# Each expert's row gathered in two halves, in an encoder step with a mixture of 16,384 rank-one experts

## What is computed

```
q = (xb @ w_pq).reshape(t, 8, 2, 128);  s = einsum('thpd,phkd->thpk', q, keys)
top 16 of each half, top 16 of the 256 sums  ->  expert (t, 8, 16), best_s
g = softmax(best_s)
h = einsum('td,thkd->thk', xb, u_emb[expert])
act = g * gelu(h)
out = einsum('thk,thkd->td', act, v_emb[expert])
```

## Time and profile before

| what | value |
| --- | --- |
| median of 3 runs | 3346.39 us (3346.24 to 3348.15) |
| the profiled execution, own time | 3345.38 us |
| its span, first to last instruction | 3343.4 us |
| busy: PE, DVE, POOL, ACT | 2485.5, 2445.1, 1397.8, 1033.0 us |
| gathers | 1,088 of 1 MB |
| mean granted TensorE clock | 0.869 |

### The profile page before, as it was taken

One profiled execution on the slowest core, in us unless ns is written; L12 is line 12 of the kernel. 1 busy time (PEld: TensorE's weight loads), 2 busy tenths in 40 slices (PEclk: granted clock), 3 DMA queues, 4 the chain that ended last, 5 costly groups with the idle time before them and its releaser, 6 DMA issues. The chain is left out here.

```text
span 3343.4 us, 41075 instructions
## 1 busy us (share of the span) xinstructions
PE 2485.5 (74%) x13555; PEld 1077.4 (32%) x13555; DVE 2445.1 (73%) x6920; ACT 1033.0 (31%) x2944; POOL 1397.8 (42%) x1266
## 2 busy tenths in 40 slices
PE   8999766777867776678767876787767766776665
PEld 4555522333322332233323332333323222222221
DVE  4888677668777777777777777777677777677885
ACT  3333233333332323332333233323332233222321
POOL 1222344344444444434444443544434444444453
PEclk9999778889887899889888988888889888888877
DMA  6223399999999999999999999999999999999997
GB/s 200 79 79 93 106 396 408 381 362 409 414 414 401 411 410 410 399 408 408 409 392 408 407 402 404 397 408 401 402 407 407 409 411 413 373 402 417 414 419 314
DMA packets 221480, 1220.90 MB, mean 365 GB/s; under 512 B 34370, under 2 KB 62738, under 8 KB 82005
## 3 DMA queue, kind: packets, MB, share of 16 engines
q0 software_dynamic: 156672, 1140.92, 84.3%
q1 hardware_dynamic: 61072, 75.91, 6.8%
q10 hardware_dynamic: 3525, 1.45, 0.2%
HBM read 1199.65 MB, written 18.55 MB: 364 GB/s over the span
## 5 line engine op out<-in xcount | busy, mean ns | idle before, releaser
L1241 POOL DMA_INDIRECT uv_rows<-in_uv_emb,experts x1088 | 1260.8, 1159 | 1629.0 <-PE ps L1349 1422.5
L1349 PE MATMUL ps<-uv_rows,diag 64*64 64x512 f32 x8704 | 1334.4, 738 | 812.4 <-ACT diag L1645 811.4
L1878 DVE CUSTOM_DVE_ANT_0 uv_rows<-uv_rows,handed 128x1024 f32<-128x1024 f32 x1088 | 1329.9, 1224 | 608.1 <-DMA uv_rows<-in_uv_emb,experts 602.8
L1349 PEld LDWEIGHTS ps<-uv_rows,diag 64*64 64x64 f32 x8704 | 322.9, 153 | 1458.5 <-ACT diag L1645 1034.0
L1637 ACT ACTIVATE gelu_c<-dots 128x2 f32<-128x2 f32 x544 | 110.5, 203 | 1606.4 <-DVE dots L1878 1606.0
L1645 ACT ACTIVATE diag<-ident_twice,act_c 128x64 f32<-128x64 f32 x1088 | 319.2, 340 | 281.5 <-DVE act_c L1895 280.3
L1309 PE MATMUL ps<-w_pq_sb,xnT_c 128*128 128x256 f32 x1152 | 339.3, 425 | 0.7 <-ACT xnT_c L1604 0.7
L1309 PEld LDWEIGHTS ps<-w_pq_sb,xnT_c 128*128 128x128 f32 x1152 | 217.9, 206 | 249.0 <-issue 226.2
L653 DVE SCALAR_TENSOR_TENSOR handed<-w_out_sb,tapsT,handed 128x128 f32<-128x128 f32 x960 | 252.8, 351 | 0.0
L590 PE MATMUL ps<-w_in_sb,w_out_sb 128*128 128x512 f32 (+1 forms) x656 | 240.7, 522 | 0.5 <-DMA w_in_sb<-in_w_in 0.5
L1895 DVE SCALAR_TENSOR_TENSOR act_c<-gelu_c,gate_inv,gate_exps 128x2 f32<-128x2 f32 x544 | 118.2, 217 | 77.0 <-ACT gelu_c L1637 57.6
(11 more groups left out here) (248 smaller groups left out, 2166.8 us busy)
## 6 DMA issues: line engine op xcount, KB each, us to landing
uv_rows<-in_uv_emb,experts POOLq DMA_INDIRECT x1088, 12.9
w_in_sb<-in_w_in SPq DMA_DIRECT2D x4, 2048.0 KB, 15.6
w_pq_sb<-in_w_pq SPq DMA_DIRECT2D x8, 1024.0 KB, 6.7
w_out_sb<-in_x_prompt SPq DMA_DIRECT2D x8, 512.0 KB, 4.3
w_out_sb<-in_w_out SPq DMA_DIRECT2D x1, 4096.0 KB, 16.4
handed<-in_x_prompt SPq DMA_DIRECT2D x8, 512.0 KB, 17.1
out<-handed SPq DMA_DIRECT2D x8, 512.0 KB, 7.9
keys_turned<-handed SPq DMA_DIRECT2D x10, 260.0 KB
```

The source lines that it names most:

```text
L1241: nc.gpsimd.indirect_dma_start(out=rows[:, m % RING, :], out_offset=None, in_=d.uv_emb[0], in_offset=bass.IndirectOffsetOnAxis(ap=experts[ ...
L1349: ins = pe.matmul(ps[dst, 2 * x + half, :], diag[src, (m + i) % DIAGS, :], rows[src, (m + i) % RING, cols], start=first, stop=last)
L1878: nc.vector.tensor_tensor_reduce(out=row, in0=row, in1=xn[:, block_of(n) % 2, :], scale=1.0, scalar=0.0, op0=ALU.mult, op1=ALU.add, accum_ ...
```

## The change

- The joined table `uv_emb` is gone; `u_emb` and `v_emb` are passed as they are. The ring of 8 slots of 8 KB becomes two rings of 8 slots of 4 KB, in the same memory.
- POOL issues two indirect DMAs a step, of 128 rows of 4 KB each: the `u` half of step `m`, which waits only for dot `m - 8`, and the `v` half of step `m - 2`, which waits until step `m - 10` has been weighed. DVE waits for the `u` half, PE for the `v` halves of its pair.
- Block 1's output projection is spread, one matmul a step, over item 4 from step 9 to item 5 step 10, and what follows from it (sum, mean square, normalisation, turned rows, queries of items 8 and 9) moves back by up to an item. The queries, scores and copies of items 8 and 9 get their own places in items 6 and 7.

```diff
@@ phase_c
-        rows = sb("uv_rows", [P, RING, 2 * s.D])
+        u_rows = sb("u_rows", [P, RING, s.D])
+        v_rows = sb("v_rows", [P, RING, s.D])
...
         def routed_in(n):
-            return chosen_in(n + 1)
+            return {6: [8], 7: [9, 10]}.get(n, chosen_in(n + 1))
@@ POOL
             def gather(n, k):
                 m = K * n + k
                 if m >= RING:
+                    pool.wait_ge(dot_done, m - RING + 1)
+                nc.gpsimd.indirect_dma_start(
+                    out=u_rows[:, m % RING, :], out_offset=None, in_=d.u_emb[0],
+                    in_offset=bass.IndirectOffsetOnAxis(ap=experts[:, slot_of(n), k:k + 1], axis=0),
+                ).then_inc(u_here[m % RING], 16)
+
+            def gather_values(m):
+                if m >= RING:
                     pool.wait_ge(weighed, (m - RING) // 2 + 1)
                 nc.gpsimd.indirect_dma_start(
-                    out=rows[:, m % RING, :], out_offset=None, in_=d.uv_emb[0],
-                    in_offset=bass.IndirectOffsetOnAxis(ap=experts[:, slot_of(n), k:k + 1], axis=0),
-                ).then_inc(here[m % RING], 16)
+                    out=v_rows[:, m % RING, :], out_offset=None, in_=d.v_emb[0],
+                    in_offset=bass.IndirectOffsetOnAxis(ap=experts[:, slot_of(m // K), m % K:m % K + 1], axis=0),
+                ).then_inc(v_here_ring[m % RING], 16)
...
                 for k in range(K):
                     gather(n, k)
+                    if K * n + k >= LAG:
+                        gather_values(K * n + k - LAG)
...
-                    if n == 5 and k == 15:
+                    if n == 6 and k == 7:
                         inverse_rms1(1)
+            for m in range(K * HEADS - LAG, K * HEADS):
+                gather_values(m)
@@ PE
             def weigh(n, k):
                 m, b = K * n + k, block_of(n)
+                for i in range(2):
+                    pe.wait_ge(v_here_ring[(m + i) % RING], 16 * ((m + i) // RING + 1))
...
-                                            rows[src, (m + i) % RING, cols], start=first, stop=last)
+                                            v_rows[src, (m + i) % RING, cols], start=first, stop=last)
...
-                    if n == 4 and 9 <= k < 13 or n == 5 and k < 4:
-                        for i in range(2):
-                            project(1, 2 * (k - 9 if n == 4 else k + 4) + i)
-                    if n == 5 and k == 6:
+                    if n == 4 and k >= 9:
+                        project(1, k - 9)
+                    if n == 5 and k == 0:
+                        project(1, 7)
+                    if n == 5 and 3 <= k < 11:
+                        project(1, k + 5)
+                    if n == 5 and k == 14:
                         gains(1, 0)
-                    if n == 5 and k == 11:
+                    if n == 6 and k == 2:
                         gains(1, 1)
...
+                    if n == 6:
+                        if 8 <= k < 12:
+                            query(8, 2 * (k - 8), 2 * (k - 7))
+                        if k == 12:
+                            turn_query(8)
+                        if k == 14:
+                            score(8)
+                        if k == 15:
+                            query(9, 0, 4)
@@ DVE
             def dot(n, k):
                 m = K * n + k
-                dve.wait_ge(here[m % RING], 16 * (m // RING + 1))
+                dve.wait_ge(u_here[m % RING], 16 * (m // RING + 1))
...
-                row = rows[:, m % RING, 0:s.D]
+                row = u_rows[:, m % RING, :]
...
-                    if n == 4 and k == 13:
+                    if n == 5 and k == 2:
                         projected(1, 0)
-                    if n == 5 and k == 4:
+                    if n == 5 and k == 12:
                         projected(1, 1)
-                    if n == 5 and k == 5:
+                    if n == 5 and k == 13:
                         mean_square1(1)
-                    if n == 5 and k == 6:
+                    if n == 5 and k == 14:
                         mean_scaled1(1)
-                    if n == 5 and k == 9:
+                    if n == 6 and k == 1:
                         normalise1(1, 0)
-                    if n == 5 and k == 12:
+                    if n == 6 and k == 4:
                         normalise1(1, 1)
```

More of the change, by code:

```diff
@@ L79, in build @@
 def build(nc, x_prompt, x_sample, cache_k, cache_v, cache_logf, state_conv, g_mix, w_in, b_f, w_dw, b_dw,
-          ln_g, ln_b, w_out, g_ffn, w_pq, sub_keys, uv_emb, g_final,
+          ln_g, ln_b, w_out, g_ffn, w_pq, sub_keys, u_emb, v_emb, g_final,
           y_prompt, y_sample, k_prompt, v_prompt, logf_prompt, conv_prompt,
           k_sample, v_sample, logf_sample, conv_sample):
-    s = sizes(x_prompt, x_sample, cache_k, w_in, w_dw, w_pq, sub_keys, uv_emb)
+    s = sizes(x_prompt, x_sample, cache_k, w_in, w_dw, w_pq, sub_keys, u_emb)
     d = Named()
@@ L86, in build @@
     d.g_mix, d.w_in, d.b_f, d.w_dw, d.b_dw, d.ln_g = g_mix, w_in, b_f, w_dw, b_dw, ln_g
-    d.ln_b, d.w_out, d.g_ffn, d.w_pq, d.sub_keys, d.uv_emb = ln_b, w_out, g_ffn, w_pq, sub_keys, uv_emb
+    d.ln_b, d.w_out, d.g_ffn, d.w_pq, d.sub_keys, d.u_emb, d.v_emb = ln_b, w_out, g_ffn, w_pq, sub_keys, u_emb, v_emb
     d.g_final, d.k_prompt, d.v_prompt, d.logf_prompt, d.conv_prompt = g_final, k_prompt, v_prompt, logf_prompt, conv_prompt
@@ L1002, in phase_c @@
         RING = 8
+        LAG = 2
         DIAGS = 6
@@ L1082, in phase_c @@
         best_ready, exps_ready, experts_ready, pair_ready = sem("best_ready"), sem("exps_ready"), sem("experts_ready"), sem("pair_ready")
-        here = [sem(f"uv_here{i}") for i in range(RING)]
+        u_here = [sem(f"u_here{i}") for i in range(RING)]
+        v_here_ring = [sem(f"v_here{i}") for i in range(RING)]
         dot_done, weighed = sem("dot_done"), sem("weighed")
@@ L1344, in weigh @@
                         pe.wait_ge(crossed_out, 2 * (b - 1) + half + 1)
-                    cols = slice(s.D + half * BANK, s.D + (half + 1) * BANK)
+                    cols = slice(half * BANK, (half + 1) * BANK)
                     for i in range(2):
@@ L1561, in _ @@
                         turn_rows(made_in(n, 3), (k - 7) // 4)
[L1562 to L1565 removed]
+                    if n == 4 and k >= 9:
[5 more added lines that the diff above has]
+                    if n == 5 and k == 14:
                         gains(1, 0)
[L1567 removed]
+                    if n == 6 and k == 2:
                         gains(1, 1)
[L1569 to L1572 removed]
+                    if n == 6 and k in (5, 7):
+                        turn_rows(1, (k - 5) // 2)
                     if left and k == 1:
                         score(left[0])
[L1575 removed]
+                    if n == 6:
[7 more added lines that the diff above has]
+                            query(9, 0, 4)
+                    elif len(routed) == 1:
                         if n > 0 and k in (1, 3, 5, 7):
@@ L1581, in _ @@
                             score(routed[0])
-                    if len(routed) == 2:
+                    if n == 7:
+                        if k == 1:
+                            query(9, 4, 8)
+                        if k == 3:
+                            turn_query(9)
+                        if k == 5:
+                            score(9)
+                    elif len(routed) == 2:
                         if k in (1, 3):
@@ L1588, in _ @@
                             score(routed[0])
+                    if len(routed) == 2:
                         if k in (9, 11):
@@ L1767, in _ @@
                         rows_out(made_in(n, 3), (i - 4) // 2)
-                    if (n, i) in ((5, 7), (6, 0)):
-                        rows_out(1, n - 5)
+                    if n == 6 and i in (3, 4):
+                        rows_out(1, i - 3)
                     head_step(n, i)
-                    if len(routed) == 1:
+                    if n == 6:
+                        if i == 5:
+                            query_out(8)
+                        if i == 6:
+                            turned_out(8)
+                        if i == 7:
+                            scores_out(8)
+                    elif len(routed) == 1:
                         if i == 4:
@@ L1778, in _ @@
                     if len(routed) == 2:
-                        if i == 2:
+                        early = 1 if n == 7 else 0
+                        if i == 2 - early:
                             query_out(routed[0])
-                        if i == 3:
+                        if i == 3 - early:
                             turned_out(routed[0])
-                        if i == 4:
+                        if i == 4 - early:
                             scores_out(routed[0])
@@ L2135 @@
 INPUTS = ["x_prompt", "x_sample", "cache_k", "cache_v", "cache_logf", "state_conv", "g_mix", "w_in", "b_f", "w_dw",
```

(2 more changed lines are left out.)

12 lines of the change are left out of this document (3 added, 9 removed).

## The result

The changed kernel takes **3545.16 us** (median of 4 runs, 3535.69 to 3551.41) against 3346.66 before on the same chip: **1.0591 times as long, 95% interval 1.0574 to 1.0608**. The profiled execution took 3549.35 us, 4.2 above the median, with a span of 3547.6. Forecast were 3470, in a range from 3405 to 3620: the direction and the new bound came out as forecast, the size was 75 us short.

A forecast was written before the change was run, and what follows sets the result against it. Transfers were taken to bound the kernel before, POOL's issues the changed one: 3345.4 + 1,088 x (2.782 - 2.667) - 2 = 3468.5, with 1.0 for the median about 3470 us, range 3405 to 3620.

The forecast's parts named there:

- The transfers bound the kernel before: Phase C before the change: about five gathers always under way, ring full, one landing every 2.667 us, so transfers limit.
- block 1's holes: DMA share gaps around block 1's projection: 11.5 of 15 us of holes; filling them gives back 12, between 0 and 15.
- The spread projection gives nothing where POOL is the bound: Block 1's projection: filling its holes gives nothing once POOL is the bound, since POOL has no slack.
- Packets of 4 KB, 114 us: Gather transfers: 4 KB rows at 403 GB/s against 8 KB at 420, 0.105 us a step, 114 us over 1,088 steps.
- The two ends, nothing and 123: Other bounds on added packets: nothing if only bytes count; 123 us at 12.6 ns for each of 9,792 packets.
- the 3445 of the rival: Rival: transfers remain the bound and POOL keeps up, 3445 us, from 3405 to 3455; chance 0.34.
- the 3405: Lower end of the transfer-bound rival and of the forecast range, given as packets at 7 ns.
- The fixed cost of a DMA: Skill's rule of about 2.0 us a DMA: 2,176 us more if nothing overlapped; given no chance of its own.
- POOL becomes the bound, 2.78 us a step, 1.09 us an issue: POOL's two issues a step, held up by dots, set the pace; forecast 3470 us, case 3455 to 3620, chance 0.49.
- What would show it: Signs: 4 KB packets near 400 GB/s at share 1.0, or holes; POOL over 75% busy; DVE's `u` wait up.
- I cost the shift at nothing: `v` halves two steps late, some 5.3 us, delaying PE's weighing: 0 us, absorbed by DVE's 603 us of gather waits.
- worse still: Rival: DVE's waits on PE come on top, 3470 + 181 = 3651 us, above 3620; chance 0.08.

The follow-up runs named there:

- e4_short_dot: Changed kernel with each dot over the first 256 of 1,024 columns, the rest left out; 3393.86 us, ratio 1.0148.
- e5_spread_short_dot: Kernel before (joined 8 KB rows) with block 1's projection spread and dots over 256 of 1,024 columns; 3331.11 us, ratio 0.9948.
- e11_weigh_later: Changed kernel, lag of two steps kept, with PE's weighing of each pair two steps later in PE's order; 3442.83 us, ratio 1.0275.
- e3_half_bytes: Changed kernel with gathers of 2 KB a row in place of 4 KB, dots whole; 3672.72 us, ratio 1.0977.
- e7_two_issues: Kernel before with each gather made two DMAs of 64 rows of 8 KB, one to each half of the partitions; 5497.87 us, ratio 1.6432.

## Why the prediction was right, and where not

- **The transfers bound the kernel before.** Right. Filling block 1's holes gives 11.5 us by itself (forecast 12), and shorter dots give another 3.5 to 7 and no more.
- **The spread projection gives nothing where POOL is the bound.** Right: whole change and halves alone differ by 1.5 us, within their spread.
- **Packets of 4 KB, 114 us.** Mis-sized: 63 measured. The two ends, nothing and 123, hold it. The 403 against 420 GB/s of the earlier trace rows came from stretches of 9 and 40 us, and the faster one was the last items, where little else moves; in the long run it is 398 in `e4_short_dot` against 407 in `e5_spread_short_dot`. With 63 the transfers alone would have ended near 3334.6 + 63 = 3398, under the 3445 of the rival, so POOL was further above the transfers than "close". Two slips in these sums change nothing: the 3405 is packets at 7.5 ns, not 7 (which makes 3400), and 2.761 / 2 - 0.30 is 1.0805, not 1.079.
- **The fixed cost of a DMA.** 1,088 more DMAs, with all their packets, cost 63 us. The 2,176 us estimated from the Trainium skill, "DMA: Bandwidth & Descriptors", section "Anatomy of one DMA — SWDGE (gpsimd) path", do not show.
- **POOL becomes the bound, 2.78 us a step, 1.09 us an issue.** The mechanism is right: an issue that starts in a dot is held until 0.8 us after it, and nearly every dot catches one. An issue takes 1.110, a step 2.852. With the lag's effect taken away it is sized well: in `e11_weigh_later`, whose dots are as even as the prediction assumed or more so, the dots pace at (3426.9 - 429.0) / 1087 = 2.758. Some luck is in that: the prediction counted three issues for any long interval; with one more for each further 1.25 us the kernel before comes to 1.951 issues a dot, and the pace to 2.73. Against the transfer-bound 3394 this hold-up by evenly spaced dots costs 49 us.
- **What would show it.** POOL is busy 2126.6 of the 2,700 us from 500 to 3200, 79%, and no longer waits for weighing, as forecast. Two signs did not come: no holes appeared in the DMA share, which stayed at 1.00 with the rate at 375 GB/s in the place of about 400, and DVE's wait for `u` halves went down, from 603 us to 440, since DVE came late itself.
- **The step that failed: "I cost the shift at nothing while DVE has its 603 us of waiting for gathers to absorb it."** It measured 80 us when the lag was taken away, 102 when the weighing was moved instead. Counted in DVE's time the sentence is true: it is busy 68% of the span, and still waits 440 us for gathers. But the cover was argued for DVE's own delay, and the price came through another engine. The late `v` halves make PE late, PE makes DVE late, the dots bunch, and bunched dots hold up POOL, which has no slack. The pace of 2.78 was worked out with the dots spaced as before, and the same change that made POOL the bound took that spacing away. The forecast of 3470 is 27 us above the 3443 measured with even dots, and has nothing for the 102: that makes the 75 by which it was short. The rival "worse still" had the first two links right, but bounded it at one step for each item, 181 us, as a delay in DVE's order.

The sum as measured: 3334.6 (whole rows, projection spread) + 63 (packets) + 49 (even dots against POOL) + 102 (uneven dots, through the lag and the place of the weighing) = 3548.6. It is a way of dividing the time, and no test: the terms are differences of the same runs, and come out at 3545.2 but for the 3.5 that short dots give the joined rows as well (3334.6 against 3331.1), from which the 63 are counted. The runs were made on several chips, on which the kernel before took 3346.1 to 3349.4 us, and single runs of one of these kernels lie 2 to 28 us apart, so none of the terms is sharper than some 5 us, and the last than some 10.

What stays open: how much of the 102 is the lag's alone, since weighing later was not tried without lag; and whether two issues a step could be had without any cost through dots, that is with DVE reading its rows in another way. It wasn't tried.

## What to carry to other kernels

Before an issuing engine's work is doubled, work out its pace with its real mean duration, the hold-ups by other engines in it, and not from the median of an undisturbed issue; and ask whether the change also moves the engine that holds it up. An engine with idle time need not absorb a delay for nothing: here the delay made its work bunch, and the price was paid by POOL, which the bunch holds up. When data are made to arrive later, move the instruction that waits for them back by as much in its queue, for everything behind it waits too: that alone gave back half of what the change lost.

## What the runs showed of the hardware that was not expected

- **A DMA share of 1.00 is no proof that the DMA engines are the limit.** In the kernel after the share is 1.00 from 500 to 3200 us at 375 GB/s, while POOL issues back to back and, with short dots, the same packets run at 398. A packet of the gathers' queue is counted with 0.846 x 16 x 3547.6 / 313,344 = 153 ns after, 148.5 by the same reckoning in `e4_short_dot` (a share of 0.858 of the queue, 3390.5 us), and 186 in `e3_half_bytes` (0.552, 3672.1 us, 174,080 packets), though the engines have the least to do there. A packet's time seems to take in some waiting. What does tell is the rate beside another kernel's, and half the bytes.
- **Two rows of 2 KB went in one packet.** `e3_half_bytes` shows 174,080 packets in the queue, 160 a step, where 256 rows and 32 semaphore packets would make 288: 128 data packets for 256 rows, and in the trace each has 4,096 B.
- **Gathers into one half of the partitions run at little over half the rate.** `e7_two_issues` moved 222 GB/s over its span, and before 365, projections and attention of the first block included in both; in phase C it is 233 against 404. Its DMA share there is 1.02 all the same. The Trainium skill, "DMA: Bandwidth & Descriptors", sections "The descriptor swizzle" and "Where 436 GB/s comes from", has partitions 0 to 63 written through one half of the ports and 64 to 127 through the other, and 435 GB/s for all 16 ports, which makes an estimated 218 for either half alone. The run is near that, as if the two gathers of a step, one to each half, had gone one after the other.
